# Experts ranked by their counts on the chip: five items of 96 rows, three of 64, whole token rows gathered and turned by TensorE

## The reference

```python
def swiglu(u, w_gate, w_up, w_down):
    return (jax.nn.silu(u @ w_gate) * (u @ w_up)) @ w_down

def moe_swiglu(u, w_router, b_router, w_gate, w_up, w_down):
    ...
    top_val, top_idx = lax.top_k(logits, TOP_K)
    gate = jax.nn.softmax(top_val, axis=-1)
    ...
    y_slots = y_slots.reshape(P, D) * slot_w[:, None].astype(u.dtype)
    return jnp.zeros((T, D), u.dtype).at[slot_tok].add(y_slots).reshape(B, L, D)
```

## Time and profile before

| | us |
|---|---|
| runs (three): lowest, median, highest | 1750.09, 1755.19, 1756.47 |
| span of the profiled execution, from its first to its last instruction | 1735.9 |
| median of the runs above that span | 19.3 |
| PE busy | 1694.7 (98%) |
| DVE, ACT, POOL busy | 676.6, 579.9, 123.7 |
| HBM read, written (MB) | 476.65, 7.40 |

### The profile page before, as it was taken

The page is one execution under the profiler, slowest core; times in us unless marked ns, Lnnn a source line. Parts: engine busy times, 40 slices in busy tenths (PEclk is TensorE's granted clock), DMA queues, the critical chain, the costliest instruction groups (busy, mean ns, idle before and its releaser), DMA issues.

```text
span 1735.9 us, 50787 instructions
## 1 busy us (share of the span) xinstructions
PE 1694.7 (98%) x22518; PEld 1414.8 (81%) x22518; DVE 676.6 (39%) x1309; ACT 579.9 (33%) x1190; POOL 123.7 (7%) x126
## 2 busy tenths in 40 slices
PE   8999999999998999999999999999999999999997
PEld 7999989999997999998877777777777777777754
DVE  7768687776646768777201010010100101001010
ACT  6778776543345777885300000000000000000000
POOL 0000001100010000002120201102011020110200
PEclk9999999999999999999999999999999999999999
DMA  6434334455454434335999999999999999999994
GB/s 227 134 98 134 122 110 146 158 178 175 161 176 162 137 120 135 126 130 167 419 413 419 401 419 408 411 419 402 418 409 411 419 401 415 403 403 416 386 418 192
DMA packets 89903, 485.98 MB, mean 280 GB/s; under 512 B 12684, under 2 KB 15660, under 8 KB 46416
## 3 DMA queue, kind: packets, MB, share of 16 engines
q1 hardware_dynamic: 83936, 476.12, 70.5%
q0 software_dynamic: 5616, 6.57, 1.6%
q10 hardware_dynamic: 144, 0.13, 0.0%
HBM read 476.65 MB, written 7.40 MB: 279 GB/s over the span
## 4 chain that ended last, share of the span: by engine, by line
PE 87%; ACT 5%; DVE 3%; DMA 2%; issue 1%; SPq 0%; POOLq 0%; POOL 0%; ACTq 0%; DVEq 0%
PE bank L1907 32%; PE bank L1924 17%; PE bank L1592 11%; PE bank L1594 10%; PE bank L1593 10%; DMA chunk<-in_w_exp 2%; ACT hi L728 1%; PE bank L1668 1%; PE bank L1708 1%; PE bank L1771 1%; PE bank L1787 1%; ACT ez L765 0%; DVE lo L1039 0%; DVE S L1346 0%; PE bank L1760 0%
## 5 line engine op out<-in xcount | busy, mean ns | idle before, releaser
L1907 PE MATMUL bank<-chunk,xt 128*32 128x256 f32 x10752 | 582.4, 379 | 1.8 <-DMA chunk<-in_w_exp 0.9
L1907 PEld LDWEIGHTS bank<-chunk,xt 128*32 128x32 f32 x10752 | 419.8, 110 | 162.5 <-DMA chunk<-in_w_exp 1.9
L1592 PE MATMUL bank<-UH,hi 128*128 128x272 f32 (+1 forms) x1024 | 309.4, 302 | 8.9 <-DVE UL L1052 5.6
L1594 PE MATMUL bank<-UH,lo 128*128 128x272 f32 (+1 forms) x1024 | 295.3, 288 | 0.0
L1593 PE MATMUL bank<-UL,hi 128*128 128x272 f32 (+1 forms) x1024 | 294.2, 287 | 0.0
L1924 PE MATMUL bank<-chunk,turned_hs 128*32 128x256 f32 x5376 | 291.7, 379 | 0.0
L1541 DVE TENSOR_TENSOR hs<-sg,bank 128x512 f32<-128x512 f32 x24 | 16.5, 688 | 693.5 <-PE bank L1907 693.5
L1039 DVE TENSOR_TENSOR lo<-raw,hi 128x1024 fp32r<-128x1024 f32 (+1 forms) x220 | 265.7, 1213 | 42.2 <-ACT hi L728 41.8
L1924 PEld LDWEIGHTS bank<-chunk,turned_hs 128*32 128x32 f32 x5376 | 208.3, 110 | 81.7
L728 ACT ACTIVATE hi<-raw 128x1024 fp32r<-128x1024 f32 (+1 forms) x220 | 229.5, 1044 | 107.1 <-PE bank L1594 105.5
L1592 PEld LDWEIGHTS bank<-UH,hi 128*128 128x128 f32 x1024 | 194.5, 190 | 19.5 <-issue 15.7
(11 more groups left out here) (335 smaller groups left out, 1775.2 us busy)
## 6 DMA issues: line engine op xcount, KB each, us to landing
chunk<-in_w_exp SPq DMA_DIRECT2D x336, 1024.0 KB, 23.5
raw<-in_w_dense SPq DMA_DIRECT2D x212, 512.0 KB, 3.3
raw<-in_w_dense SPq DMA_DIRECT2D x8, 384.0 KB, 3.2
wuq<-in_w_uq SPq DMA_DIRECT2D x2, 1024.0 KB, 8.4
hT<-in_tokens SPq DMA_DIRECT2D x4, 272.0 KB, 3.5
wukv<-in_w_ukv SPq DMA_DIRECT2D x2, 512.0 KB, 9.0
y_rows<-acc SPq DMA_DIRECT2D x1, 1024.0 KB, 18.7
u_rows<-u_strips SPq DMA_DIRECT2D x1, 1024.0 KB, 19.2
```

What stands on the lines that cost most here:

```text
L1592: MM(ps, h, xh_, start=first, stop=False)
L1594: return MM(ps, l, xh_, start=False, stop=last)
L1907: ins = MM(bank[b_ + t // 2][q * ROWS:(q + 1) * ROWS, t % 2 * DQ:(t % 2 + 1) * DQ], xt[:, t, kt0 + r, :], w_[:, (r * NQ + q) * DQ:(r * NQ ...
```

## The change

Before: up to 13 items of 96 rows, in the order of the experts. After: the experts are ranked on the chip by their number of places. Expert 0 always comes first, for its chunks are loaded before the counts are known. The five first in rank get an item of 96 rows each (N_BIG), the three others an item of 64 rows each (N_SMALL, two row tiles). What doesn't fit goes to extra items of 96 rows, up to five, between the two groups. PE and POOL, SP, ACT and DVE run a loop over the large items and then the three small ones: PE in a second hardware loop, the other engines in code written out three times.

Of an item, the row gather is a single indirect DMA of whole rows of 4 KB into up to 96 partitions (`gidx` has the token numbers, loaded on their own), instead of three of quarter rows. PE turns these rows with eight transposes into two banks after chunk 29 of the item before (TURN_AT = GU + 1), and waits there for the gather (`x_next`); DVE copies the result to `xt`. The strips of u and the zeroed rows of `u_rows` are no longer made or stored. The selection for the first item comes from the ranks directly, ahead of the slots, and ACT copies both halves of its `xt`. POOL gathers no further rows after the last item.

```diff
-MAX_ITEMS = 13
-PAIR_W = 2 * NQ
+N_BIG, MAX_EXTRA = 5, 5
+MAX_BIG = N_BIG + MAX_EXTRA
+SMALL_T = 2
...
-TURN_AT = 36
+TURN_AT = GU + 1
...
             sp.wait_ge(zeroed, 2)
-            sp.dma_start(u_whole_rows[SEQ:SEQ + P, :], xtok[:]).then_inc(u_stored, 16)
             sp.dma_start(y_whole[SEQ:SEQ + P, :], xtok[:]).then_inc(h_stored, 16)
+            sp.wait_ge(utok_made, 4)
+            sp.dma_start(u_rows.rearrange("(b p) d -> p b d", p=P), utok[:]).then_inc(u_stored, 16)
             sp.wait_ge(acc_loaded, 4)
...
+            sp.wait_ge(items_ready, 1)
+            sp.wait_ge(table_ready, 1)
...
+            for j in range(N_SMALL):
+                e = sp.value_load(it_i[0:1, SMALL_AT + j:SMALL_AT + j + 1], min_val=0, max_val=NE - 1)
+                for k in range(ITEM):
+                    sp.wait_ge(chunk_done, n_before * ITEM + ((j + 1) * ITEM + k - MRAW + 1))
+                    load_chunk(e, k)
...
+            def next_rows(i, at, n_t):
+
+                n = n_t * ROWS
+                pool.dma_start(gidx[0:n, :], slots[bass.ds(at, n), 2 * NQ:2 * NQ + 2]).then_inc(index_loaded, 16)
+                pool.wait_ge(index_loaded, i * 16 + 16)
                 pool.wait_ge(x_back, i + 1)
                 pool.sem_inc(row_step, 1)
-                for t in range(N_T):
-                    pool.indirect_dma_start(xg[:, t, :], None, u_rows[:],
-                                            bass.IndirectOffsetOnAxis(rows[:, N_T + t, 0:1], 0)).then_inc(rows_landed, 16)
+                pool.indirect_dma_start(xg[0:n, :], None, u_rows,
+                                        bass.IndirectOffsetOnAxis(tokens[0:n, 0:1], 0)).then_inc(rows_landed, 16)
+                pool.wait_ge(rows_landed, i * 16 + 16)
+                pool.sem_inc(x_next, 1)
...
-            for b in range(2):
-                A_(u_strips[:, b, :, :, :], utok[:, b, :].rearrange("p (k q f) -> p q k f", q=NQ, f=ROWS),
-                   ACT.Copy).then_inc(u_split, 1)
...
+            st(STT(key, cnt, float(NE), order, ALU.mult, ALU.add))
+            st.wait()
+            st(TT(ahead[:], key.rearrange("p (o f) -> p o f", o=1).broadcast_to([P, NE, NE]),
+                  key.rearrange("p (e o) -> p e o", o=1).broadcast_to([P, NE, NE]), ALU.is_gt))
+            st.wait()
+            st(E.tensor_reduce(rank, ahead[:], AX.X, ALU.add))
+            st.wait()
+            st(TS(small, rank, N_BIG - 0.5, None, ALU.is_gt))
...
                     if k == TURN_AT:
-                        dve.wait_ge(rows_landed, i * (16 * N_T) + 16 * N_T)
-                        dve.wait_ge(chunk_done, i * ITEM + GU)
-                        E.transpose(xt[:].rearrange("p t k r -> p (t k r)"),
-                                    xg.rearrange("p t c -> p (t c)")).then_inc(x_back, 1)
...
+                        dve.wait_ge(x_turned, i + 1)
+                        for half in range(2):
+                            ins = CP(xt[:, :, 4 * half:4 * half + 4, :],
+                                     bank[6 + half][:, 0:4 * CAP].rearrange("p (k t r) -> p t k r", k=4, r=ROWS))
+                        ins.then_inc(x_back, 1)
...
                         for r in range(2):
-                            for t in range(N_T):
+                            for t in range(n_t):
                                 for q in range(NQ):
...
                     ins.then_inc(chunk_done, 1)
+                    if k == TURN_AT:
+
+                        pe.wait_ge(x_next, i + 1)
+                        for half in range(2):
+                            for c in range(4):
+                                ins = TR(bank[6 + half][:, c * CAP:(c + 1) * CAP],
+                                         xg[:, (4 * half + c) * P:(4 * half + c + 1) * P], ident[0:CAP, 0:CAP])
+                        ins.then_inc(x_turned, 1)
+
+            with nc.Fori(0, n_big, engines=bass.OrderedEngineSet([pe.engine]), hint_back_edge=True,
+                         head_slot={pe.engine: LOOP_SLOT}) as i:
+                item(i, i * N_T + N_T, N_T)
+            with nc.Fori(0, N_SMALL, engines=bass.OrderedEngineSet([pe.engine]), hint_back_edge=True,
+                         head_slot={pe.engine: LOOP_SLOT}) as j:
+                item(n_big + j, n_big * N_T + j * SMALL_T + N_T, SMALL_T)
```

More of the change, by code:

```diff
@@ L707, in _ @@
             pool.wait_ge(out_stored, 16)
-            for t in range(N_T):
+            for t in range(SMALL_T):
                 pool.wait_ge(last_made, t + 1)
@@ L1022, in _ @@
                         act.wait_ge(rows_added, i + 1)
-                        for t in range(N_T):
+                        for t in range(n_t):
                             A_(ysb[:, t, :], bank[4 + t // 2][:, t % 2 * DQ:(t % 2 + 1) * DQ], ACT.Copy, scale=pairs[:, t, 1:2]).then_inc(y_made, 1)
+            with nc.Fori(0, n_big, engines=bass.OrderedEngineSet([act.engine]), hint_back_edge=True) as i:
+                activate(i, N_T)
+            for j in range(N_SMALL):
+                activate(n_big + j, SMALL_T)
         @block.vector
@@ L1465, in _ @@
             TT(top[:, :, 2], top[:, :, 1], top[:, :, 0], ALU.subtract).then_inc(router_diff, 1)
-            nb, end, start = (R(9 + n)[:, 0, :] for n in range(3))
+            key, rank, small, cap, base, over, extra, start, ended, turn_by = (R(7 + n // 2)[:, n % 2, :]
+                                                                               for n in range(4, 14))
             at = rt[:, 0:2, :, :]
@@ L1470, in _ @@
             dve.wait_ge(ranked, 1)
-            cnt = bank[5][:, 16:24]
-            st(TT(nb, cnt, least, ALU.is_gt))
+            cnt = got[:, 2 * NE:3 * NE]
+            pos = got[:, 0:2 * NE].rearrange("p (b e) -> p b e", b=2)
+            each = lambda x: x.rearrange("p (o e) -> p o e", o=1).broadcast_to([P, 2, NE])
+            CP(got[:], bank[5][:, 0:3 * NE]).then_inc(got_ranks, 1)
+            dve.wait_ge(got_ranks, 1)
+            for b in range(2):
+                ins = TS(sel[:, b, :], iota, pos[:, b, 0:1], cs[:, b, 0:1], ALU.is_equal, ALU.mult)
+                if b == 0:
+                    st(ins)
+                else:
+                    ins.then_inc(sel_ready, 1)
@@ new lines, in _ @@
+            st(TT(over, cnt, cap, ALU.subtract))
+            st(TT(base, rank, cap, ALU.mult))
+            st.wait()
+            st(TS(extra, over, 0.0, None, ALU.is_gt))
+            st.wait()
+            st(STT(extra, over, float(CAP), extra, ALU.is_gt, ALU.add))
+            st.wait()
+            st(E.tensor_tensor_scan(start[:, 1:NE], extra[:, 0:NE - 1], extra[:, 0:NE - 1], 0.0, ALU.add, ALU.bypass))
+            st.wait()
+            st(TT(ended, start, extra, ALU.add))
+            st.wait()
@@ new lines, in _ @@
+            st(TS(nit_i[:, 0:1], ended[0:1, NE - 1:NE], float(N_BIG), None, ALU.add))
+            TS(nit_i[:, 1:2], ended[0:1, NE - 1:NE], float(N_BIG - 1), None, ALU.add).then_inc(items_ready, 1)
+            number = MC[0:1, 0:NE]
+            down = number.rearrange("p (n o) -> p n o", o=1).broadcast_to([1, NE, NE])
+            across = lambda x: x[0:1, :].rearrange("p (o e) -> p o e", o=1).broadcast_to([1, NE, NE])
+            st(TT(iit[:, 0, :, :], down, across(rank), ALU.is_equal))
+            st(TT(iit[:, 1, :, :], down, across(ended), ALU.is_ge))
@@ new lines, in _ @@
+            st(STT(base, small, float(SMALL_BASE - N_BIG * SMALL_CAP), base, ALU.mult, ALU.add))
+            st(TT(gs, pos, each(cap), ALU.is_ge))
+            st.wait()
+            st(TT(turn_by, base, cap, ALU.add))
+            st(TT(tmp, pos, each(base), ALU.add))
+            st.wait()
+            st(STT(turn_by, start, float(CAP), turn_by, ALU.mult, ALU.subtract))
+            st.wait()
+            st(TS(turn_by, turn_by, float(N_BIG * CAP), None, ALU.add))
+            st.wait()
+            st(TT(gs, gs, each(turn_by), ALU.mult))
@@ L1481, in _ @@
+            st.wait()
+            st(TT(gs, gs, tmp, ALU.add))
             st.wait()
@@ L1888, in _, with item @@
             pe.wait_ge(x_front, 1)
-            pe.wait_ge(items_ready, 2)
-            n_items = pe.value_load(nit_i[0:1, 0:1], min_val=1, max_val=MAX_ITEMS)
-            with nc.Fori(0, n_items, engines=bass.OrderedEngineSet([pe.engine]), hint_back_edge=True,
-                         head_slot={pe.engine: LOOP_SLOT}) as i:
+            pe.wait_ge(items_ready, 1)
+            n_big = pe.value_load(nit_i[0:1, 0:1], min_val=N_BIG, max_val=MAX_BIG)
+            def item(i, made, n_t):
                 for k in range(ITEM):
```

193 lines of the change are left out of this document (98 added, 95 removed).

## The result

| | before | after |
|---|---|---|
| median, us (runs) | 1753.3 (4) | 1731.45 (4) |
| lowest, highest | 1750.09, 1756.47 | 1729.96, 1732.49 |
| profiled execution: span, device time | 1735.9, not known | 1730.5, 1732.17 |

The ratio is 0.9874, with a 95% interval of 0.986 to 0.9889: 22 us faster, twice what was forecast, and outside the range of 1738 to 1753. The two profiles by themselves differ by 5.4 us only. The execution profiled after took 1.7 us more than its span. The first profile of before is 1735.9 beside runs of 1750 and more, and the prediction had put the 19.3 us between them outside the span. Span against span, it had forecast 1735.9 - 10.7 = 1725.2 for the changed kernel; the span after is 1730.5, so by this measure the change brought less than forecast, not more.

What follows compares the result with a forecast made beforehand. PE was taken to bound the expert stage, with DMA within 2%; with smaller items the late DMA half decides. 6.9 us of stream made 9.4 at PE's end, plus 1.3 of tail: 10.7, so 1744.5 us, range 1738 to 1753.

Steps and rivals of the forecast that it cites:

- the last of the sum: Whole run: 10.7 us gained of the 1735.9 span, the median's 19.3 above the span kept, so 1744.5 us.
- PE is the bound, with 1.7 us lost to DMA: Expert stage before: eight items of 108.78 us of PE make 870.2 of the stage's 872.0 us.
- by now behind: Expert stage before: DMA within 2% of PE, a chunk's issue to landing growing from 16.4 to 28.5 us.
- PE's end ... 9.4 gained: End of expert stage: last chunk lands at 1713.4, one small chunk follows, PE ends at 1715.1 against 1724.5.
- (a) to (c) and the tail: DMA stream: zeroed rows not stored 1.2, smaller adds 1.6, fewer and smaller gathers 2.0 us; one final scatter fewer, 1.3.
- (d) Fetches: Late half of the DMA engines: PE's instruction packets fall by a third in three items, counted as 2.1 us.
- That a row is fetched whole changes no byte; ... I count 0: Gathers, under term (c): whole-row fetching counted as 0, bounds 0 and 0.5 us an item.
- What costs nothing: Turns (5.5 us in the large items) and second PE loop's entry (1 us) covered by lead; first gather up to 1.2 earlier.
- 2 was wrong: Rival, small items: PE's clock falls to the slower side; all at 1.2 GHz gives 1867 us. Chance 0.06.
- extra item: Rival 3, routing: over 64 rows in a small-group expert or another ranking, nine items, +98 us, 1853. Chance 0.02.
- Rival 4: Expert stage: DMA is faster when asked to, three small items save 109 - 5.5 us, 1652. Chance 0.02.
- Rival 1: DMA stream: its end hardly moves, fetch and store savings fail, 1749 us. Chance 0.36, with the first mechanism's small gains.

Runs made afterwards that it cites:

- b_again: The kernel before, run once more unchanged: median 1754.29 us, ratio 1.0003.
- two floors: PE leaves out the third row tile of every item, DMA traffic kept: the kernel before then takes 1728.6 us, the changed one 1726.4.
- b_pe1: The kernel before with PE at one row tile an item, two left out: 1713.35 us, ratio 0.9773.
- b_gather1: The kernel before with one of the three indirect gathers of each item: 1740.98 us, ratio 0.9928.
- a_small3: The changed kernel with its three small items at three row tiles instead of two: 1757.52 us, ratio 1.0024 to the kernel before.
- b_pe2_again: The kernel before with PE at two row tiles an item, third left out, a second run: 1728.84 us, ratio 0.9857.

## Why the prediction was wrong

**The step that failed** is the last of the sum, with the view that it was made against: "The runs' median is 1755.19, 19.3 above that span; with the same distance 1744.5 us." The distance is 1.7 us in b_again, and at most 3.3 in any run. The sum thus took 1735.9 us for what an ordinary execution does inside its span, and put the missing 14 us outside it. They lie in the expert stage, as stops of PE that the first profile doesn't have and that b_again does. (The first profile's own device time isn't on record.) With the right distance the sum would have come to some 1727 us, 4.5 too low: the gain from the profiled execution was put too high, and the time that an ordinary one had to lose was left out. Against b_again the spans fall into these parts:

| part, us | before (b_again) | after | difference |
|---|---|---|---|
| up to the first expert matmul | 851.8 | 853.5 | +1.7 |
| five items | 552.0 | 551.4 | -0.6 |
| switch of loops | 0 | 5.2 | +5.2 |
| last three items | 334.7 | 309.7 | -25.0 |
| tail | 11.3 | 10.7 | -0.6 |
| span | 1749.8 | 1730.5 | -19.3 |

**"PE is the bound, with 1.7 us lost to DMA", and DMA "by now behind".** The first half was right. The second was right only of that one execution, in which PE's pace of 108.78 was just over what DMA could follow. At the ordinary 110 us an item the median landing is 18 to 20 us after issue from 1300 us to the end, not 28.5, so six or seven chunks lie ready, and PE ends 19 us after the stream. (Six or seven is an estimate: 14 buffers less 18 to 20 us at 2.6 a chunk.) This lead is what the small items use up, and the first of them does so: 92.2 us, then 110.3 and 107.2, whose mean is near the 108.4 that I gave to the stream. The prediction had named small items under 105 us as a sign that it was wrong; their mean is 103.2.

**"PE's end ... 9.4 gained".** The mechanism was right: from the sixth item on the end is the stream's, and one small chunk follows it (1717.84 to 1719.8). The size wasn't. Of the 9.4, 6.9 was to come from a lighter stream and 2.5 from PE's distance to it. The stream's last bytes hardly moved, from about 1719 to 1718; PE's distance to it gave some 17 us. The terms (a) to (c) and the tail, 4.8 and 1.3 in my sum, come to some 2 us between the two floors; which of the terms was too large isn't known.

**"(d) Fetches", 2.1 us on an inferred late half.** The inference held, by b_pe1. At 0.19 us a packet the 13 packets fewer of the page (179 to 166) are 2.4 us, an estimate. Against it stand six packets more in the other row (q14, 28 to 34), from 1309 us on.

**"That a row is fetched whole changes no byte; ... I count 0".** Right for bytes, wrong for PE: three gathers in a row cost PE 1.1 us an item and more in the last, one costs nothing. In before that is worth 12 us (b_gather1): some 1.1 in each of seven items and 4 in the last. I had looked at POOL's instructions as work of POOL and of DMA alone. In the changed kernel this pays for the turns (0.95 an item, 7.6), for the switch (5.5, and 2.3 for the clock behind it) and for the later start (0.7): 16.1 together against 12, and everything but the two tiles was measured at 3.8 us of loss (a_small3).

**"What costs nothing".** The turns are hidden by DMA, as said. The switch was put at 1 us and is 5.2, hidden too. PE does not stop in chunk 29. The start is 1.7 us later in this pair instead of 1 earlier: PE's wait is for DVE (2.2 us at L1592), which runs through its longer chain before it takes up the loop. That wait I had not seen. The start scatters, though: over all profiles PE's first expert matmul comes at 851.8 to 856.7 us in the kernels made from before, and at 852.3 to 853.5 in those made from after, so neither a gain nor a loss of the start is shown.

**The rivals.** The clock was 0.97 to 1.00 in the windows of the small items, with PE at 1.73 us of work in 2.5; only behind the stop of 5.2 us was it at 0.50 for some 7 us, so 2 was wrong. There was no extra item. Rival 4 wasn't met either: the stream in the last three items runs at 403 to 413 GB/s, as before; it is the lead that makes them short. The Trainium skill's limit for HBM per core of about 358 GB/s (DMA: Bandwidth & Descriptors, Specifications) is exceeded in the windows of the changed kernel, with 405 and 413 GB/s. Rival 1 had the stream's end right, which hardly moved, and the time wrong.

## What to carry to other kernels

Before a sum is made, put the profiled execution's span beside its own time; where the time isn't known and the median lies more than a few us above the span, profile again, since the missing part may be the stage that the change touches. Where PE is the bound by 1%, its gain ends where the loads' lead is used up: what a smaller tile wins is the distance from the last landing to PE's end, and that can be read directly (here 19 us). And a loop body on PE that must be fetched anew each pass is DMA traffic on half of the engines: here a body a third as long, which isn't fetched anew, was worth 15.5 us against one of two thirds in a kernel bound by DMA.

## What was not expected of the hardware

- Three indirect gathers 1.3 us apart leave a PE at full pace with four or five instructions each 0.7 us, 1.1 us lost; six indirect DMAs cost about 6 us in the last item. One, or three adds 1.9 us apart, cost nothing. Why the first profile shows none of it, with the same three gathers, stays open.
- Instruction packets of a PE body of 4032 instructions come 16 an item and load one half of the DMA engines; of a body two thirds as long 10 or 11 an item, of one a third as long none after the first pass. Where between one and two thirds the limit lies wasn't tried. ACT's and DVE's bodies, with 1010 instructions more between them, brought ten packets of 8 KB an item, where before they brought none until the last item.
- With PE on one tile and waiting for DMA the granted clock went back and forth between its two levels of 2.4 and 1.2 GHz (0.50 throughout from 1040 to 1080 us), 0.63 to 0.71 in the mean of stretches of 100 us; with two tiles, 0.98 to 1.00:

```profile
1000.00:1100.00 100.00, 66.10 (x616) 21.73 (x620) 8.69 (x15) 3.80 (x9) 10.18 (x10) 0.63 1.02 414
```

```profile
1000.00:1100.00 100.00, 74.98 (x1216) 37.74 (x1216) 8.69 (x15) 3.81 (x9) 10.19 (x10) 0.98 1.02 412
```

The first is b_pe1, the second b_pe2_again, which was nearer to rival 2 than the changed kernel came.
